# Odd layer of a two-block network: values projected as feature rows beside each head, gates moved behind the first head

## What is computed

```python
def odd_layer(x, norm_g, w_in, w_out, qn, kn, ..., subln_g, cos, sin, lambda_init):
    h = rms_norm(x, norm_g)
    proj = h @ w_in                                # 1024 -> 4096
    q, k, v, gate = split(proj)                    # 1024 features each
    q, k = rms_norm over each 64 features          # 8 heads, 2 halves each
    q1, q2, k1, k2 = rope(...)
    v = v.reshape(b, s, 8, 128)
    # per head and block of 128 queries, keys up to the query's chunk
    a = softmax(q1 k1 / 8) - lam * softmax(q2 k2 / 8)
    o = a @ v
    o = rms_norm(o, subln_g) * (1 - lambda_init)
    y = (o * silu(gate)) @ w_out
    return x + y
```

## Time and profile before

| | us |
|---|---|
| median of 3 runs | 2012.36 |
| lowest, highest | 2011.19, 2012.70 |
| the profiled execution's own time | 2011.72 |
| its span in the profile | 2009.9 |
| odd layer, border to scan | about 292 to 632 |

### The profile page before, as it was taken

How to read it: one execution, slowest core, us unless ns; L and a number is a source line. 1 busy time by engine, 2 the same in 40 slices (tenths; PEclk the granted TensorE clock), 3 DMA queues, 4 the chain that set the end, 5 groups by cost and what they waited for, 6 DMA issues and landing times.

```text
span 2009.9 us, 26575 instructions
## 1 busy us (share of the span) xinstructions
PE 1936.9 (96%) x10008; PEld 1607.4 (80%) x10008; DVE 1042.4 (52%) x1934; ACT 990.9 (49%) x1737; POOL 946.4 (47%) x1236
## 2 busy tenths in 40 slices
PE   6999999989989999999999999999999999999997
PEld 5778888866778877777788888888878888888886
DVE  4366543378743677766736564412546574444214
ACT  5466634367743565556526444422555464444323
POOL 4542355554535444444364555555452445555553
PEclk9999999999999999999999999999999999999999
DMA  5321223331222222222132223233221223223332
GB/s 186 95 69 43 61 76 95 90 89 53 84 62 86 74 74 74 75 74 82 56 105 85 100 95 102 94 92 99 77 70 55 74 74 105 95 95 97 95 95 71
DMA packets 55200, 169.36 MB, mean 84 GB/s; under 512 B 7072, under 2 KB 13856, under 8 KB 54944
## 3 DMA queue, kind: packets, MB, share of 16 engines
q1 hardware_dynamic: 54784, 166.92, 26.5%
q10 hardware_dynamic: 288, 0.74, 0.1%
HBM read 158.72 MB, written 2.10 MB: 80 GB/s over the span
## 4 chain that ended last, share of the span: by engine, by line
PE 77%; DVE 12%; ACT 4%; POOL 3%; issue 2%; DMA 1%; SPq 0%; ACTq 0%; DVEq 0%; POOLq 0%
PE ps L1839 19%; PE ps L1842 19%; PE ps L1840 19%; PE ps L1899 2%; POOL wl L2569 2%; PE ps L1851 2%; PE ps L1854 2%; PE ps L1852 2%; PE ps L1884 2%; DVE tmp L2392 1%; PE ps L1892 1%; DVE s_xbc L2371 1%; PE ps L1864 1%; PE ps L1866 1%; PE ps L1867 1%
## 5 line engine op out<-in xcount | busy, mean ns | idle before, releaser
L2569 POOL TENSOR_TENSOR wl<-st,wh 128x256 fp32r<-128x256 f32 (+1 forms) x1180 | 877.2, 776 | 998.7 <-ACT wh L2005 998.2
L2005 ACT ACTIVATE wh<-st 128x1024 fp32r<-128x1024 f32 (+2 forms) x311 | 314.2, 1011 | 502.2 <-PE ps L1842 441.7
L1839 PE MATMUL ps<-xh,wh 128*128 128x512 f32 x1368 | 555.5, 406 | 1.6 <-DVE tmp L2259 1.6
L1842 PE MATMUL ps<-xh,wl 128*128 128x512 f32 x1368 | 534.3, 391 | 0.8 <-POOL wl L2569 0.8
L1840 PE MATMUL ps<-xl,wh 128*128 128x512 f32 x1368 | 533.2, 390 | 0.0
L1839 PEld LDWEIGHTS ps<-xh,wh 128*128 128x128 f32 x1368 | 257.3, 188 | 60.0 <-issue 8.3
L1842 PEld LDWEIGHTS ps<-xh,wl 128*128 128x128 f32 x1368 | 256.7, 188 | 56.9 <-POOL wl L2569 1.7
L1840 PEld LDWEIGHTS ps<-xl,wh 128*128 128x128 f32 x1368 | 257.5, 188 | 49.8 <-issue 2.6
L2526 DVE SCALAR_TENSOR_TENSOR tmp<-ps,vec,tmp 128x510 f32<-128x510 f32 (+1 forms) x176 | 131.3, 749 | 209.8 <-ACT tmp L2184 206.9
L2484 DVE SCALAR_TENSOR_TENSOR res<-res,ps 128x512 f32<-128x512 f32 (+1 forms) x37 | 22.7, 615 | 220.9 <-PE ps L1842 212.2
L1839 PE MATMUL ps<-fa_h,wh 128*128 128x512 f32 x308 | 120.6, 392 | 0.0
(11 more groups left out here) (276 smaller groups left out, 3508.7 us busy)
## 6 DMA issues: line engine op xcount, KB each, us to landing
st<-in_f_up SPq DMA_DIRECT2D x88, 512.0 KB, 3.2
st<-in_s_xbc SPq DMA_DIRECT2D x32, 512.0 KB, 3.5
st<-in_f_dn SPq DMA_DIRECT2D x32, 512.0 KB, 3.5
st<-in_o_fm SPq DMA_DIRECT2D x24, 512.0 KB, 3.5
st<-in_e_fm SPq DMA_DIRECT2D x21, 512.0 KB, 3.5
st<-in_s_z SPq DMA_DIRECT2D x16, 512.0 KB, 3.5
st<-in_s_out SPq DMA_DIRECT2D x16, 512.0 KB, 3.5
tmp<-tmp SPq DMA_DIRECT2D x100, 64.0 KB, 2.0
```

Of the source, the lines that this page charges most:

```text
L1839: e.matmul(u.bank.ap, hi, x.h[:, kk, :], start=first, stop=False)
L1842: e.matmul(u.bank.ap, lo, x.h[:, kk, :], start=False, stop=last).then_inc(S["mm"], 1)
L2005: e.activation(P.mem["wh"][w.m % NWR][:, 0:w.n], P.mem["stage"][w.m % NSTAGE][:, 0:w.n], ACT.Copy).then_inc(S["w_hi"], 1)
L2569: t = e.tensor_tensor(P.mem["wl"][w.m % NWR][:, part], P.mem["stage"][w.m % NSTAGE][:, part], P.mem["wh"][w.m % NWR][:, part].bitcast(F32) ...
```

## The change

The value weight is laid out like those of queries, keys and gates and stands behind them in the same array, as units 24 to 31. The value of head h is projected as a unit of its own with features on the partitions, right behind the query and the key of that head. The new v_post copies the bank on ScalarE, transposes it in four blocks on TensorE and copies the result on VectorE into the head's columns of v. tv now has one entry for each head; attend waits for the entry of its head, and so does the product with the values. The border takes query, key and value of head 0 in place of gates 0 to 2. Gates 0 and 1 go beside head 1, gates 2 and 3 beside head 3; all eight are now brought by the copy and the pair of Silus. The wait of prep for the first four gates is gone.

```diff
+    gates.beside = {1: [0, 1], 3: [2, 3], 5: [4], 6: [5], 7: [6, 7]}
-    tv = []
+    tv = [None] * 8
...
-    def v_post(b, half, u):
-        t = yield ("v_in", v[:, b, half * 512:(half + 1) * 512], u, over)
+    def v_post(h, u):
+        vf = yield from P.taken(P.tmp)
+        t = yield ("va_in", vf, u)
         u.bank.release(t)
-        tv.append(t)
+        bank = yield from P.taken(P.aux)
+        t = yield ("va_t", bank, vf, t)
+        vf.release(t)
+        tv[h] = yield ("va_out", v[:, :, h * 128:(h + 1) * 128], bank, [t, over])
+        bank.release(tv[h])
+
+    def first(j, u):
+        if j < 2:
+            prep(0, "qk"[j], u)
+        else:
+            P.start(4, v_post(0, u))
 
     def stream():
-        yield from P.proj_border_g(x, [w[j] for j in range(3)], lambda j, u: P.start(4, gates.first(j, u)))
-        P.start(4, gates.first(3, (yield from P.proj_g(x, [w[3]]))))
-        yield from prep(0, 8, "od_qn", "q", qs)
-        yield from prep(0, 16, "od_kn", "k", ks)
-        for half in range(2):
-            us = []
-            for r in (P.at, P.at, P.at, P.ob):
-                us.append(Unit((yield from P.taken(r))))
-            yield from P.proj_tok_g(x, [T["o_v"][half, j] for j in range(4)], us)
-            for b in range(4):
-                P.start(5, v_post(b, half, us[b]))
+        yield from P.proj_border_g(x, [w[8], w[16], w[24]], first)
         for h in range(1, 8):
-            yield from prep(h, 8 + h, "od_qn", "q", qs)
-            u = yield from prep(h, 16 + h, "od_kn", "k", ks)
+            prep(h, "q", (yield from P.proj_g(x, [w[8 + h]])))
+            prep(h, "k", (yield from P.proj_g(x, [w[16 + h]])))
+            P.start(4, v_post(h, (yield from P.proj_g(x, [w[24 + h]]))))
             for j in gates.beside.get(h, ()):
...
-        t = yield ("pv", ob, i * 128, 128, [pt.ready, tv], [cols(pt.ap, b) for b in range(nb)],
+        t = yield ("pv", ob, i * 128, 128, [pt.ready, tv[h]], [cols(pt.ap, b) for b in range(nb)],
...
-        while len(tv) < 8:
-            yield lambda: len(tv) == 8
         for h in range(8):
-            while len(got.get(h, ())) < 2:
-                yield lambda: len(got.get(h, ())) == 2
+            while len(got.get(h, ())) < 2 or tv[h] is None:
+                yield lambda: len(got.get(h, ())) == 2 and tv[h] is not None
...
-    r["o_fm"] = fm(cat([o[:, 3072:4096], o[:, 0:2048]], 1))
-    r["o_v"] = tm(o[:, 2048:3072], 2)
+    r["o_fm"] = fm(cat([o[:, 3072:4096], o[:, 0:3072]], 1))
```

More of the change, by code:

```diff
@@ L1132, in odd_layer, with prep @@
     got = {}
[L1134 to L1137, removed]
+    def prep(h, key, u):
+        gain, pool = ("od_qn", qs) if key == "q" else ("od_kn", ks)
         P.start(4, P.qk_prep_g(u, (P.V(gain), tgain), True, key, pool,
                                lambda dst: got.setdefault(h, {}).__setitem__(key, dst)))
-        return u
-    def v_post(b, half, u):
-        t = yield ("v_in", v[:, b, half * 512:(half + 1) * 512], u, over)
+    def v_post(h, u):
+        vf = yield from P.taken(P.tmp)
+        t = yield ("va_in", vf, u)
         u.bank.release(t)
-        tv.append(t)
-    def stream():
-        yield from P.proj_border_g(x, [w[j] for j in range(3)], lambda j, u: P.start(4, gates.first(j, u)))
-        P.start(4, gates.first(3, (yield from P.proj_g(x, [w[3]]))))
-        yield from prep(0, 8, "od_qn", "q", qs)
-        yield from prep(0, 16, "od_kn", "k", ks)
-        for half in range(2):
-            us = []
-            for r in (P.at, P.at, P.at, P.ob):
-                us.append(Unit((yield from P.taken(r))))
-            yield from P.proj_tok_g(x, [T["o_v"][half, j] for j in range(4)], us)
-            for b in range(4):
-                P.start(5, v_post(b, half, us[b]))
+        bank = yield from P.taken(P.aux)
[8 more added lines that the diff above has]
+            P.start(4, v_post(0, u))
+    def stream():
+        yield from P.proj_border_g(x, [w[8], w[16], w[24]], first)
         for h in range(1, 8):
-            yield from prep(h, 8 + h, "od_qn", "q", qs)
-            u = yield from prep(h, 16 + h, "od_kn", "k", ks)
+            prep(h, "q", (yield from P.proj_g(x, [w[8 + h]])))
+            prep(h, "k", (yield from P.proj_g(x, [w[16 + h]])))
+            P.start(4, v_post(h, (yield from P.proj_g(x, [w[24 + h]]))))
             for j in gates.beside.get(h, ()):
```

## The result

The changed kernel takes 2017.78 us in the median of 10 runs (2014.40 to 2018.91), the kernel before 2012.53 us in 10 runs beside them (2011.19 to 2016.66). The ratio is 1.002, 95% interval 1.0011 to 1.0029: slower by 0.2%, about 4 us (the medians lie 5.3 apart). The forecast was 2018.0 in 2007 to 2027. The profiled execution took 2018.69 us, its span is 2016.8 us.

What follows compares the result with a forecast made beforehand. TensorE was taken as the bound, busy 96% of the span. The profiled 2011.7 + 4.7 added work - 0.5 - 2.3 + 0.7 + 1 + 2 gave 2017.3 us; the median lies 0.6 higher, so 2018, range 2007 to 2027.

Steps and rivals of the forecast that it cites:

- Exchanged work: Value projection's 64 steps in the other form, weight bytes, splits and eight VectorE copies cost the same: 0.
- Transposes: Eight added groups of four value transposes on TensorE, 0.49 us a group: 3.9 us.
- ten extra runs: Additional runs of projection matmuls beginning after something else, up to the scan, 0.08 us each: 0.8 us.
- Waits on o_pr: Probability transposes in the heads waiting for a tile's last VectorE step: -0.5 us, the planner closing the distances again.
- Product with the values: In the heads, its waits for the copy of the transposed probabilities shrink: -2.3 us, bounds 0 and -3.7.
- Keys: Scores waiting for keys at pair starts, heads 2 and 4 at the edge: +0.7 us net, bounds -1.4 and +8.
- Border: Where the norm of x arrives, banks free later and TensorE waits for ScalarE: +1 us, bounds -1 and +4.
- Gate blocks: Four ScalarE gate blocks among the heads instead of two, partly covered by a reduce: +2 us, bounds 0 and 7.6.
- Clock: Low clock at 585 to 590 us, worth 1.5 us, stays as the later order is the same: 0.
- no change: Rival: waits in the heads fall by about what the added work costs, with VectorE's load; 2011 us, chance 0.26.
- Faster: Rival: filler takes away two thirds of the heads' remaining 15 us of waits; 2007 us, chance 0.18.
- Clearly slower: Rival: pair starts and gate blocks cost their bounds, +8 and +5; 2027 us, chance 0.14.

Runs made afterwards that it cites:

- e5: Changed kernel with the planner given longer lengths for the two mixes, same instructions in another order: 2011.88 us, ratio 0.9991 to the kernel before.
- e1: The changed kernel untouched, run and profiled again: 2015.95 us, ratio 1.0014 to the kernel before.
- e12: The kernel before untouched, run again for a second profile: 2014.54 us.
- e7: Changed kernel with a second pair of table loads behind each of the odd layer's four gate blocks, unknown to the planner: 2028.94 us, ratio 1.0075.
- e10: Changed kernel with second pairs of table loads at gate blocks, now in the planner's list, the even layer's late gates included: 2022.85 us, ratio 1.0048.
- e8: Changed kernel with four unread matmuls on constants, two at the last head's transposes, two before the later output weights' wait: 2014.20 us, ratio 1.0004.
- e11: The kernel before with four unread matmuls on constants at the last head and before the later output weights' wait: 2012.98 us, ratio 0.9994.
- e2: Changed kernel with gates 0 to 3 back at the border, ahead of head 0's query, key and value: 2021.02 us, ratio 1.0036.

## Why the prediction came out right

The total was hit, 2018.0 against 2017.78; of the steps some were right and two errors cancelled. That it was hit so closely is luck: the sum lay too high up to the last head and had nothing behind it, and the second run of the same kernel had its median at 2015.95.

- **Exchanged work, price 0:** nothing in the windows speaks against it.
- **Transposes, 3.9 us:** 3.4 by the group's starts, 2.4 by the doubled groups (0.30 us each). The 0.41 us of the even layer held for one group there and is 0.35 here. The ten extra runs at 0.8 us were not measured alone. The Trainium skill's 275 ns for one transpose ("TensorE: Matmul & The Clock Gate", Part 4: PE-mode transpose), 8.8 us by that, is no price here: the trace has 0.35 us for four.
- **Waits on o_pr, -0.5:** 9.3 and 8.0 us in the two profiles before, 6.8 and 7.6 after, so -1.5. The wait stayed at the lower edge of 7 to 10, and e5 supports the reasoning by distances. The account took the chains as they were; but the last mix at width 128 takes 453 ns in the mean in the changed kernel (452 in e1) where it took 585 (583 in e12), so the chains got shorter too, and how much of the 1.5 us is that was not tried.
- **Product with the values, -2.3:** all 3.7 us went, the lower bound. Its cover of 0.68 us was enough everywhere.
- **Keys, +0.7:** heads 2 and 4 do wait, and head 0, as three small waits of 1.5 us together; before it was one of 1.4 (two of 1.6 in e12). So the net is nothing. In the changed kernel:

```profile
399.46 0.41 PE L1882 MATMUL ps<-kz,qz 128*128 128x128 f32 x2 [0.49 <-DVE kz L2537]
...
467.25 0.41 PE L1882 MATMUL ps<-kz,qz 128*128 128x128 f32 x2 [0.88 <-DVE kz L2537]
```

- **Border, +1:** from 292 us to the first score TensorE waits 3.6 us where it waited 1.7 up to 331 before: +1.9, inside its bounds; the new part is 1.7 us for the banks that L2257 frees, and 0.3 us for ScalarE.
- **Gate blocks, +2:** at most 0.4 us of wait follows a block in the changed kernel, so about 0. But the ground given for a small price, a reduce that covers 2.4 us of the block, was not the point: e7 and e10 show that the planner's knowledge of the block's length covers it, with next to no slack. What came instead was not on the list: 3.7 us of waits on ScalarE past the border, two for squares (1.2 us), one for an exponential of the last head (1.4) and one for a copy (1.2). The last is the change's own, the value's transposes behind the query's two copies in ScalarE's queue. ScalarE, then TensorE:

```profile
456.25 1.28 ACT L2200 ACTIVATE qz<-tmp 64x512 fp32r<-64x512 f32 x2 [3.53 <-DVE tmp L2262]
457.56 0.60 ACT L2033 ACTIVATE tmp<-ps 128x512 f32<-128x512 f32 x1
```

```profile
458.21 0.66 PE L1911 MATMUL ps<-const,tmp 128*128 128x128 f32 x4 [1.17 <-ACT tmp L2033]
```

- **Clock, 0:** this step failed. It read that TensorE's order behind the last head is the same and took the low clock as part of it. Behind the last head the low clock took 1.7 us in both profiles before, 3.4 and 5.1 after, and what it costs depends on where it lies: all of it ahead of the wait for a weight before, 3.1 us behind that wait after. It is worth 2.4 to 3.0 us, the difference of the last stretch. With the low clock kept out of both (e8 and e11) the ratios to the kernel before are 1.0004 and 0.9994, 0.1% or 2 us apart with intervals that overlap, and the last stretches are equal.
- **The sum:** the forecast put 5.6 us between border and last head and none behind. The profiles have 1.6 to 3.2 us there and 2.4 to 3.0 behind. Without the wait for the weight, TensorE's waits are 20.4 and 20.1 us before, 19.0 and 19.8 after, some 0.8 less; with the added TensorE work, 2.4 to 3.4 us of transposes and up to 0.8 of extra runs, that makes 1.6 to 3.4, which agrees with the first piece.
- **Rivals:** "no change" needed the waits to follow VectorE's load; they fell by 1.5 us where its load fell by 25 us in the window. "Faster" fell with it. "Clearly slower" had the gap of a pair and the blocks as places: the keys' gap held, and the blocks would have done it had they been one pair of loads longer than planned.

**Left open:** why e2 is 4 to 5 us over the changed kernel, 2 of them behind the scan; whether the changed kernel's own mix lengths would do as well as those of e5; why the low stretch behind the last head is some 7 to 10 us long in the changed kernel and 3.5 in e5, where TensorE pauses no less; and how much of the change's own 2 us is the ten extra runs.

## What to carry to other kernels

On a kernel whose order is a planner's, look for the operation whose measured length differs most from the planner's table before moving work: here longer lengths for two operations were worth 4 to 5 us, at least as much as the change cost, and in the other order the same numbers did harm. The measured means moved with the order too (585 against 453 ns for one operation), so measure and try anew on every order. An engine's block is hidden only as long as the planner knows its length. A low-clock stretch has a price only where no wait follows it: ask of each whether a wait for another engine ends after it, and count it again once the change has moved it.

## What the runs showed of the hardware

TensorE's granted clock drops to its lower level (0.50 in the windows, 1.2 GHz) for a few microseconds in places of an otherwise busy kernel: in the kernel before at 585, 1065 and 1635 us in both profiles, at 300 and 1435 in one of them only; the last 10 us of the program, in which TensorE has almost nothing left to do, are apart from this. Such a stretch behind a pause can be had away by work on constants in the pause: 3.5 us of matmuls nobody reads made the changed kernel about 2 us faster, with 2.5 to 2.9 us off its last stretch, and the kernel before no slower. From scan to end the low clock took 1.7 us in the changed kernel and e11, leaving the last 10 us out, and 5.1 in e5, and the stretch is 1378.8, 1378.4 and 1379.4 us long. The six profiles without a low stretch near 1435 us have 1378.4 to 1378.8 us there, the eight with one 1379.3 to 1380.8: its 1.7 us go with 0.5 to 1.1 us there. The 1380.8 is e2 alone, and the rest of its 2 us has no cause shown.
